# Five buffers of turned keys, and the small softmax and the weights placed between other steps' operations, in the sample attention of layer b

## The reference

```python
def layer_b_sample(x, pool, page_table, buf, ...):
    q_c, q_r, rows, wrows, gates, z = project_b(rms_norm(x, norm_g), w_in, q_gain, k_gain, pos)
    past = pool[page_table].reshape((N, past_len) + pool.shape[2:])
    full = jnp.concatenate([past, rows], axis=1)
    o_c, o_s = nsa_cmp_sel(q_c, q_r, full, pos, k_gain, pe, w1, w2)
    o_w, new_buf = window_sample(q_r, wrows, buf, WIN_B)
    y = x + nsa_output(o_c, o_s, o_w, gates, z, w_out)
```

## Time and profile before

| | |
|---|---|
| median of 3 runs | 1354.34 us (1353.39 to 1355.47) |
| the profiled execution | 1350.71 us, span 1348.9 us |
| mean granted clock of PE | 0.957 of full speed |
| busy over the span | PE 1222.2 us (91%), DVE 463.0 (34%), ACT 394.1 (29%), POOL 295.5 (22%) |
| DMA over the span | 197.21 MB |

### The profile page before, as it was taken

The page is one execution under the profiler, slowest core; times in us unless marked ns, Lnnn a source line. Parts: engine busy times, 40 slices in busy tenths (PEclk is TensorE's granted clock), DMA queues, the critical chain, the costliest instruction groups (busy, mean ns, idle before and its releaser), DMA issues. The chain is left out here.

```text
span 1348.9 us, 20946 instructions
## 1 busy us (share of the span) xinstructions
PE 1222.2 (91%) x7869; PEld 792.6 (59%) x7869; DVE 463.0 (34%) x1205; ACT 394.1 (29%) x947; POOL 295.5 (22%) x423
## 2 busy tenths in 40 slices
PE   3999999999898889699999997999988879797898
PEld 2576576677687743355446465565557767585543
DVE  1333333000455521244121013666742343434321
ACT  5111111111566400512112013666643333333210
POOL 1455554000000000167232001554530000000000
PEclk9999999999999989799998986999989989898999
DMA  6034334582312996336677932302026847343801
GB/s 234 30 147 165 158 136 180 195 290 98 99 44 80 303 295 182 127 125 218 244 230 283 297 55 73 112 2 63 1 58 177 203 125 189 116 135 99 214 9 59
DMA packets 87646, 197.21 MB, mean 146 GB/s; under 512 B 9770, under 2 KB 39258, under 8 KB 86394
## 3 DMA queue, kind: packets, MB, share of 16 engines
q1 hardware_dynamic: 87546, 195.87, 45.7%
HBM read 185.16 MB, written 73.28 MB: 192 GB/s over the span
## 5 line engine op out<-in xcount | busy, mean ns | idle before, releaser
L446 PE MATMUL bank<-la_region,la_hT 128*128 128x512 f32 x640 | 283.2, 599 | 1.7 <-PEq L164 1.7
L446 PEld LDWEIGHTS bank<-la_region,la_hT 128*128 128x128 f32 x640 | 173.1, 275 | 96.2 <-issue 46.7
L1247 PE MATMUL bank<-lb_region,lb_oT 128*128 128x512 f32 (+2 forms) x528 | 210.2, 558 | 2.1 <-PEq L164 1.7
L1247 PEld LDWEIGHTS bank<-lb_region,lb_oT 128*128 128x128 f32 (+1 forms) x528 | 96.5, 199 | 104.4 <-issue 103.3
L1439 PE MATMUL bank<-cs_chunks_turned,lb_region 128*128 128x252 f32 x512 | 125.9, 392 | 4.7 <-ACT cs_hidden L1503 3.9
L1439 PEld LDWEIGHTS bank<-cs_chunks_turned,lb_region 128*128 128x128 f32 x512 | 96.0, 197 | 18.9 <-issue 5.7
L1492 DVE COPY cs_chunks_turned<-bank 64x512 f32<-64x512 f32 x64 | 43.7, 683 | 97.1 <-PE bank L1424 97.1
L1494 ACT ACTIVATE cs_chunks_turned<-bank 64x512 f32<-64x512 f32 x64 | 38.0, 593 | 114.4 <-PE bank L1424 114.3
L494 POOL TENSOR_TENSOR pa_swapped<-pa_normed,pa_tables 128x256 f32<-128x256 f32 (+1 forms) x60 | 50.2, 856 | 77.3 <-DVE pa_normed L513 77.3
L1828 POOL TENSOR_SCALAR ab_probs<-ab_probs,ab_rec,lb_gates 128x128 f32<-128x128 f32 (+3 forms) x96 | 58.2, 623 | 33.8 <-DVE ab_rec L1874 33.6
L465 ACT ACTIVATE pa_squares<-bank 128x512 f32<-128x512 f32 (+1 forms) x30 | 16.0, 533 | 162.4 <-PE bank L446 154.8
(11 more groups left out here) (334 smaller groups left out, 1808.1 us busy)
## 6 DMA issues: line engine op xcount, KB each, us to landing
la_region<-in_a_w_in SPq DMA_DIRECT2D x10, 2048.0 KB, 8.0
out_new_dil_s<-in_cache_dil SPq DMA_DIRECT2D x8, 2032.0 KB, 13.5
lb_region<-in_b_w_in SPq DMA_DIRECT2D x7, 2048.0 KB, 9.0
la_region<-in_cache_dil SPq DMA_DIRECT2D x13, 1024.0 KB, 15.8
lb_qp<-in_cache_nsa_paged SPq DMA_DIRECT2D x32, 256.0 KB, 4.7
lb_region<-in_cache_nsa_paged SPq DMA_DIRECT2D x32, 256.0 KB, 4.0
sb_sel_keys<-in_cache_nsa_paged SPq DMA_DIRECT2D x64, 128.0 KB, 3.8
sb_sel_values<-in_cache_nsa_paged SPq DMA_DIRECT2D x64, 128.0 KB, 4.1
```

What stands on the lines that cost most here:

```text
L446: ins = nc.tensor.matmul(U[u.v % 3][:, :], permuted(hT[:, k, :], u.g, u.t), W[:, u.c % 2, k, :], start=(k == 0), stop=(k == KC - 1))
L1247: ins = nc.tensor.matmul(U[u.v % 3][0:u.R, 0:n], hT[:, k, u.t * P:u.t * P + u.R], W[:, u.c % 2, k, 0:n], start=(k == 0), stop=(k == KC - 1))
```

## The change

It does six things.

1. A fifth `kT` buffer, over the constant `causal`; a copy of group x waits for products five groups back in the same manner.
2. On PE the two transposes and two products of the way from the small softmax to the block mask move one group later each (behind u5, u7 and u9 instead of u4, u6 and u8).
3. On DVE, in `scores`, the weights of the small softmax stand behind the copy of u0, its two scalings behind the copy of u2, instead of ahead of all copies. In pairs 1 and 2 the key norm of the step before (`key_squares`, `key_scale`) moves from that step to the same places.
4. In steps 7, 11 and 15 PE issues quarter, quarter, turn, quarter, turn, quarter, turn, tokens, turn.
5. In these steps ACT exponentiates the selected keys, copies the first turn, exponentiates the window keys and copies the rest; then comes `act_finish` and last `silu`, which stood the other way round.
6. In these steps DVE scales the selected keys behind the copy of the first turn and the window keys behind that of the second, instead of behind all four.

```diff
+    def pe_products_first(self, pe, y):
+        for part in ("products", "products", "turn", "products", "turn", "products", "turn", "tokens", "turn"):
+            if part == "products":
+                self.hidden(pe, y - 1, self.n_products % 4)
+                self.n_products += 1
+            elif part == "turn":
+                self.turn(pe, 4 * y + self.n_turns % 4)
+                self.n_turns += 1
+            else:
+                self.tokens(pe, y - 2)
...
                 self.copy_out(dve, x, 0)
-        if y >= 2 and y % 2 == 0 and y // 2 - 1 < self.nI:
-            self.keys(dve, y // 2 - 1)
+        if keys and y >= 2 and y % 2 == 0 and y // 2 - 1 < self.nI:
+            self.key_squares(dve, y // 2 - 1)
+            self.key_scale(dve, y // 2 - 1)
...
-        kT = [own_kT[:, 0, :], own_kT[:, 1, :], S.const("cos")[:, 0:512], S.const("sin")[:, 0:512]]
+        kT = [own_kT[:, 0, :], own_kT[:, 1, :], S.const("cos")[:, 0:512], S.const("sin")[:, 0:512], S.const("causal")]
+        NKT = len(kT)
...
+        behind_masks = {HEAD + 4 * pair: pair for pair in range(NPAIR) if HEAD + 4 * pair < 2 * NB}
+        behind_merge = {HEAD + 4 * pair + 3: pair + 1 for pair in range(NPAIR) if HEAD + 4 * pair + 3 < 2 * NB + 2}
...
-                    nc.tensor.matmul(bank[rows, :], q, kT[x % 4], start=True, stop=True, skip_group_check=True).then_inc(m["mul"], 1)
+                    nc.tensor.matmul(bank[rows, :], q, kT[x % NKT], start=True, stop=True, skip_group_check=True).then_inc(m["mul"], 1)
...
-                        if u == 4:
+                        if u == 5:
                             pe.wait_ge(m["pcmp"], 2 * pair + 2)
...
-                        if u == 6:
+                        if u == 7:
                             pe.wait_ge(m["cmpTc"], pair + 1)
...
-                        if u == 8:
+                        if u == 9:
                             pe.wait_ge(m["covc"], pair + 1)
...
+                interleave((scores, lambda pair: None, lambda pair: None, turns, output, merge),
+                           lambda y: (C.pe_products_first if y in behind_masks else C.pe_step)(pe, y), unit, rest)
...
                 engine.wait_ge(m["tr"], x + 1)
-                if x >= 4:
-                    engine.wait_ge(m["mul"], x // 4 * 4)
+                if x >= NKT:
+                    engine.wait_ge(m["mul"], (x - NKT) // 4 * 4 + 4)
                 if x % 2 == 0:
-                    nc.vector.tensor_copy(kT[x % 4], B[4][:, :]).then_inc(s_ev[0], 1)
+                    nc.vector.tensor_copy(kT[x % NKT], B[4][:, :]).then_inc(s_ev[0], 1)
                 else:
-                    nc.scalar.activation(kT[x % 4], B[5][:, :], ACT.Copy).then_inc(s_ev[1], 1)
+                    nc.scalar.activation(kT[x % NKT], B[5][:, :], ACT.Copy).then_inc(s_ev[1], 1)
...
+                def least(pair):
+                    if pair not in behind_masks.values():
+                        exp_sel(pair)
+                        exp_win(pair)
+                def step(y):
+                    if y not in behind_masks:
+                        C.act_step(act, y)
+                        return
+                    exp_sel(behind_masks[y])
+                    C.copy_out(act, 4 * y, 1)
+                    exp_win(behind_masks[y])
+                    for x in range(4 * y + 1, 4 * y + 4):
+                        C.copy_out(act, x, 1)
+                    C.act_finish(act, y - 2)
+                    C.silu(act, y - 1)
...
                     dve.wait_ge(m["small"], pair + 1)
                     lowest(B[3][:, 64:64 + NCMP_S], 0, m["lcmp"])
-                    dve.wait_ge(m["ecmp"], pair + 1)
-                    weigh(pair, 0)
-                    if pair:
-                        dve.wait_ge(m["pv"], pair)
-                    nc.vector.tensor_scalar(pcn[:, 0:NCMP_S], pc[:, 0:NCMP_S], rec[:, 0:1], None, ALU.mult).then_inc(m["pcmp"], 1)
-                    nc.vector.tensor_scalar(pc[:, 0:NCMP_S], pc[:, 0:NCMP_S], wt[:, 0:1], None, ALU.mult).then_inc(m["pcmp"], 1)
+                    late_keys = [y // 2 - 1 for y, behind in behind_merge.items() if behind == pair]
                     for u in range(0, NU, 2):
                         evacuate(dve, NU * pair + u)
+                        if u == 0:
+                            for it in late_keys:
+                                C.key_squares(dve, it)
+                            dve.wait_ge(m["ecmp"], pair + 1)
+                            weigh(pair, 0)
+                        if u == 2:
+                            for it in late_keys:
+                                C.key_scale(dve, it)
+                            if pair:
+                                dve.wait_ge(m["pv"], pair)
+                            nc.vector.tensor_scalar(pcn[:, 0:NCMP_S], pc[:, 0:NCMP_S], rec[:, 0:1], None, ALU.mult).then_inc(m["pcmp"], 1)
+                            nc.vector.tensor_scalar(pc[:, 0:NCMP_S], pc[:, 0:NCMP_S], wt[:, 0:1], None, ALU.mult).then_inc(m["pcmp"], 1)
...
+                def weights(pair):
+                    if pair not in behind_masks.values():
+                        weigh_sel(pair)
+                        weigh_win(pair)
+                def step(y):
+                    if y not in behind_masks:
+                        C.dve_step(dve, y, keys=y not in behind_merge)
+                        return
+                    C.copy_out(dve, 4 * y, 0)
+                    weigh_sel(behind_masks[y])
+                    C.copy_out(dve, 4 * y + 1, 0)
+                    weigh_win(behind_masks[y])
+                    C.copy_out(dve, 4 * y + 2, 0)
+                    C.copy_out(dve, 4 * y + 3, 0)
...
-                interleave((scores, least, weights, turns, output, merge), lambda y: C.dve_step(dve, y), unit, rest)
+                interleave((scores, least, weights, turns, output, merge), step, unit, rest)
```

More of the change, by code:

```diff
@@ L1394, in __init__ @@
         self.last = 2 * self.nI + 3
+        self.n_products = self.n_turns = 0
         CH = 16 * max(items)
@@ L1538, in pool_program, with key_squares @@
                                     ALU.pow).then_inc(m["rstd"], 1)
-    def keys(self, dve, it):
+    def key_squares(self, dve, it):
         nc, m = self.S.nc, self.m
@@ L2052, in interleave @@
             rest(v)
+        behind_masks = {HEAD + 4 * pair: pair for pair in range(NPAIR) if HEAD + 4 * pair < 2 * NB}
+        behind_merge = {HEAD + 4 * pair + 3: pair + 1 for pair in range(NPAIR) if HEAD + 4 * pair + 3 < 2 * NB + 2}
+        assert all(y % 2 for y in behind_masks)
         ident = S.const("ident")
@@ L2266, in scores, with exp_sel @@
                         evacuate(act, NU * pair + u)
-                def least(pair):
+                def exp_sel(pair):
                     act.wait_ge(m["lsel"], pair + 1)
@@ L2271, in least, with exp_win @@
                                          accum_out=den[:, 1:2]).then_inc(m["esel"], 1)
+                def exp_win(pair):
                     act.wait_ge(m["lwin"], pair + 1)
@@ L2287, in _ @@
                 nothing = lambda pair: None
-                interleave((scores, least, nothing, turns, nothing, nothing), lambda y: C.act_step(act, y), nothing, rest)
+                interleave((scores, least, nothing, turns, nothing, nothing), step, nothing, rest)
             @block.gpsimd
@@ L2346, in least, with weigh_sel @@
                     lowest(pwin[:, :], 2, m["lwin"])
-                def weights(pair):
+                def weigh_sel(pair):
                     dve.wait_ge(m["lwin"], pair + 1)
@@ L2352, in weights, with weigh_win @@
                     nc.vector.tensor_scalar(psel[:, :], psel[:, :], wt[:, 1:2], None, ALU.mult).then_inc(m["psel"], 1)
+                def weigh_win(pair):
                     dve.wait_ge(m["ewin"], pair + 1)
```

6 lines of the change are left out of this document (4 added, 2 removed).

## The result

The changed kernel takes **1320.82 us** (median of 4 runs, 1315.35 to 1326.04) against 1353.90 for the kernel before beside it: ratio 0.9753, 95% interval 0.9712 to 0.9794. 1323 us was said, with a range of 1316 to 1331. The profiled execution took 1321.83 us, span 1320.0. The four runs lie 10.7 us apart, and their mean granted clock goes the same way: 0.969 in the fastest, 0.956 in the slowest.

What follows compares the result with a forecast made beforehand. PE's idle time and half clock, chiefly waits for DVE's key copies, bound the kernel. Seven pieces won 32.1 us, less 0.9 for the clock: 31.2, giving 1319.5 profiled, 1323 us against the median; range 1316 to 1331.

Steps and rivals of the forecast that it cites:

- Scores of pairs 1 and 2: First key transpose to first compress product behind the masks: 19.96 and 19.76 us become 13.0, 7.0 and 6.8 won.
- rival 2: Key transposes never hold the clock, so whole score pieces run at half; only the masks' 10.9 won, 1343 us; chance 0.03.
- The last hole: Late in scores, five block-mask operations in DVE's queue hold the copy of u10 until 11.85; last products start at 12.0.
- Masks: Pairs 0 to 2, first compress product behind the masks to next compress step: 13.0 us each; 4.2, 2.5, 4.2 won.
- The new silu hole: Next compress step's first product on PE waits for ACT's silu, now last in its queue: 1.2 us added per masks piece.
- Rival 4: No silu hole: values' copy and table load come sooner, 3 x 1.2 comes back; gain 35, 1319 us; chance 0.10.
- Scores of pair 0: Key norm stays ahead, first copy only 1.2 us earlier, half clock lasts as before: 15.9 us, 2.8 won.
- Scores of pair 3: No key norm in front; first copy at about 0.6, first products at 3.8, piece 12.1 us: 4.6 won.
- The allowance of 0.9: Clock loss from idle PE in the first six groups of pairs 1 to 3: a fifth of 1.45 us each, 0.9 together.
- Rival 1: One fall of the clock per pair in pairs 1 to 3: gain 27.7, 1327 us; chance 0.15.
- Rival 3: The fifth buffer is no help; holes of 0.95 and 1.05 stay in four pairs: 8 us less, 1331 us; chance 0.06.
- rival 5: Output weights land late ahead of unit 0; slower than before only if they take 50 us; chance 0.02.

Runs made afterwards that it cites:

- the old masks: Changed kernel with steps 7, 11 and 15 in their old order on PE, ACT and DVE, against the kernel before: 1330.11 us, ratio 0.9842.
- the key norm: Changed kernel with the key norm of step 6 also moved into the scores of pair 0, against the kernel before: 1314.86 us, ratio 0.9711.
- the early table: Changed kernel plus step 6's key norm in pair 0's scores, an unread small silu loading the table early, silu and values' copy before ACT's last copy: 1312.62 us.
- the small softmax alone: Kernel before with DVE's new order in the scores and PE's small products a group later, four buffers, old masks: 1339.57 us, ratio 0.9906.
- silu before the last copy: Changed kernel with silu ahead of ACT's copy of the last turn in steps 7, 11 and 15, values' copy last: 1318.88 us, ratio 0.9751.
- the two last improvements: Added to the changed kernel: step 6's key norm in pair 0's scores, and ACT's reordered steps 7, 11, 15 with silu's table loaded early: 1312.62 us.

## Why the prediction was right

By its own steps:

- **Scores of pairs 1 and 2**: 7.0 and 6.8 said, 7.1 and 6.9 measured. The placing held: u2 1.53 after u0 (1.4 said), u3 2.74 (2.9), first products 4.67 (4.75), last ones 11.87 (12.0). The holes are 0.44 and 0.58 where about 0.5 and 1.0 stood. Taking the parts out shows the causes: without the new order of DVE the hole is 3.98, without the buffer 0.60 and 0.72. One remark was off: "Holes of some 3.5 us remain" goes with the 9.4 us of PE work in rival 2, where the profile has 10.91 us of busy PE in the 12.87, and holes of 0.44, 0.58 and 0.78. The sum did not rest on it, since it placed the starts by the copies.
- **The last hole** of 0.78 was put down to the block mask's five operations ahead of the copy of u10. They do hold it (the copy runs 1149.50 to 1150.19), but ACT's copy of u11 ends at 1150.13; moving the block mask alone would have won some 0.06 us. That was argued from the rows, not run.
- **Masks**: 4.2, 2.5 and 4.2 said, 4.3, 2.6 and 4.3 measured. The second turn came 5.74 after the piece's start (5.8), the last waited 0.17 (0.45), the weights' transposes not at all. The old order alone brings back 17.20, 15.52 and 17.21.
- **The new silu hole**: 1.2 said, 1.17 measured, three times. Rival 4, that it would not come, is refuted.
- **Scores of pair 0**: 2.8 said, 2.0 measured. The step that failed is "I take the half clock of before as staying there for as long": before, the granted clock between 1082 and 1084 was back at 0.85 on average, after it was still 0.50 there, and it stayed so for about twice as long. Without the hole the piece is 12.87, so hole and clock together cost 3.83: 1.7 of it is idle time (2.70 against 0.44 and 0.58), which leaves some 2.1 for the clock where 1.45 stood. With the same hole the piece took 16.14 to 16.86 in other runs.
- **Scores of pair 3**: 4.6 said, 3.3 measured. The step mis-sized is again the clock: 12.1 was placed at full clock, and 12.22 or 12.23 came in three runs where the clock stayed at 1.00 (the old masks, the key norm, the early table), 13.36 here where it fell, and 12.97 to 13.39 in four others where it fell too. The allowance of 0.9 was spread over pairs 1 to 3; in fact it fell on pairs 0 and 3, with 0.8 and 1.1. That 31.2 came so near to 30.6 is thus in part luck: these two together are twice the allowance, the other five pieces won 0.5 more than placed, and pair 3's clock does not fall in every execution.
- **Rival 1**, a fall in each of pairs 1 to 3, came true in pair 3 alone. **Rival 2** falls: pairs 1 and 2 stand at 1.00, through 12 transposes alone too (1141 to 1143). The sentence of the Trainium skill (TensorE: Matmul & The Clock Gate, Part 4: PE-mode transpose) that transposes do not bring full clock is against the earlier trace rows, where the clock rose from 0.50 to 1.00 with transposes alone. **Rival 3** falls by the run with four buffers, **rival 5** by unit 0, which waits for nothing (1250.63, no bracket).
- **The median**: the forecast added 3.63, the distance of the profiled execution of before from its median. For the changed kernel the profiled execution was 1.0 above its median, so this step was 4.6 too high; the execution itself was 2.3 longer than the 1319.5 said (0.6 in the pieces, 1.7 in the stages ahead). The two go opposite ways and leave the 2.2 us by which 1323 missed the median, so that nearness is luck; the test of the working is the stretch. The 30.6 us of the stretch are 28.9 between the profiles and 33.1 between the medians.

## What to carry to other kernels

Where one engine's copies feed another, ask of each copy what stands ahead of it in its own queue and which buffer it needs; tiny work that is due later belongs behind the first copies, and an order that puts two groups of products ahead covers a long wait of two other engines. When a move puts an activation of another function last, its table load joins the path: place it, or a tiny activation that triggers it, in idle time. Compare variants between two fixed points inside the stage: there 3 us are plain that the medians hide. Read the granted clock of each piece with it, since one fall that comes in some executions only was worth 1.1 to 1.7 us here.

## What the runs showed of the hardware

- The same hole does not always cost the same. Behind 2.60 us at the second turn the masks took 17.2 us or 15.5 us, in other pairs in other runs (17.21, 15.53, 17.21 before; 15.53, 17.22, 17.21 with the small softmax alone), and the rows show granted clocks of 0.50 and of 1.00. The Trainium skill (TensorE: Matmul & The Clock Gate, Part 1: The HAM clock gate) says that the number of slow products at a kernel's start differs from run to run of one kernel; these pieces show the like behind a hole in mid-kernel, with 1.7 us of difference.
- The clock also fell with no long hole ahead. In pair 3 the longest hole of PE just ahead of the scores is 0.81 us and the one within their first groups 0.44; all the same the granted clock fell to 0.50 in five of the eight runs with the new order of the scores and five buffers (12.97 to 13.39 us), and in three it stayed at 1.00 (12.22 or 12.23). What decides it stays open.
- What lies ahead of the stretch ended at different times: pair 0's first transpose came between 1070.22 us (old masks) and 1076.98 (silu before the last copy), and neither of these two runs changes the code ahead of it. These 6.8 us are not much less than the two last improvements together (175.18 to 166.57, 8.6 us).
- A table load of 1.28 us showed no idle time before or behind it, at 1154.07 with the small silu 0.01 us behind it as in the earlier trace rows. The extra 1.38 us that the Trainium skill (ScalarE: Activation LUTs, What ACT_TABLE_LOAD costs) gives for a drain shows in no row here; with it the early load would, as an estimate from that figure, have ended at some 1156.7, and the third copy started at 1155.60.
